# Every fourth low half of the weights by a negated copy and an adding transfer, in a transformer block written out without loops

## The chip, the core and the metric

The kernel runs on one core of one Trainium2 chip. The metric is the time of one execution in microseconds (us), the median of three runs. The core has TensorE (PE) for matmuls, VectorE (DVE), ScalarE (ACT), GpSimd (POOL) and SyncE (SP), which here only issues transfers. Each engine runs its own list of instructions in order; they meet at semaphores. Transfers run on the core's 16 DMA engines, issued by SP or by GpSimd.

## The reference

One block of a transformer on 256 tokens of width 2048, all in float32:

```python
xn = rms_norm(h, norm_mix_g[l])
proj = xn @ w_in[l]                       # 2048 x 8448
q_a, k_a, v_a, q_b, k_b, v_b, g_a, g_b = jnp.split(proj, offsets, axis=-1)
o_a = mixer_a(...)                        # 16 heads on 2 kv heads, window, sink, t5 bias
o_b = mixer_b(...)                        # 16 heads, chunked, relative bias
merged = sigmoid(g_a) * (o_a @ w_branch_a[l]) + sigmoid(g_b) * (o_b @ w_branch_b[l])
h = h + merged @ w_out[l]
hn = rms_norm(h, norm_ffn_g[l])
h = h + (silu(hn @ w_ffn_gate[l]) * (hn @ w_ffn_up[l])) @ w_ffn_down[l]   # width 5632
```

## The kernel before

All weights are read once from HBM, some 250 MB. To keep float32 accuracy each product is taken in three matmuls: weight and activation are each split into a high half (`w_hi`, `xT_hi`: the value rounded to the type float32r) and a low half (`w_lo`, `xT_lo`: what is left), and TensorE adds hi x hi, lo x hi and hi x lo in PSUM (lines 948, 949, 950).

The work is a list of jobs made by `plan`, one for each 512 columns of a weight (the first, `kv`, has 256). A job is a row of *pieces*: a piece is 2 x 128 rows of the weight by the job's columns, for TensorE 12 matmuls (2 row blocks, 2 token tiles, 3 products). There are 464 pieces, numbered through (`p`). Two pieces are a *chunk* of 1 MB, the unit of loading. For every piece each engine does its step, and then what `follow` hangs on that place in the list (taking sums out of PSUM, norms, gates, splitting the activations):

- SP loads chunk c into slot c % 4 of `raw` (line 394), when the low half of the last piece of chunk c - 4 is made (`lo_ready`).
- ScalarE copies the piece from `raw` to slot p % 4 of `w_hi` (`split_hi`, line 494), when TensorE is through with piece p - 4 (`piece_used`).
- VectorE subtracts: `w_lo` = `raw` - `w_hi` (`split_lo`, line 648).
- TensorE waits for `lo_ready` at the start of the piece and multiplies.

So `w_hi` and `w_lo` have four slots, and a piece may be made while TensorE works on the three before it. The jobs alternate between two pairs of PSUM banks. Between pieces TensorE also turns finished tiles (`turn_set`, line 877), and from the first `ga` job on (piece 72) it does attention for 34 pieces: on even pieces `scores` and `turn_probs`, on odd ones `values`, with exponentials on ScalarE (line 594) and maxima and scaling on VectorE. GpSimd has little to do: it issues eight small loads at the start and one small store (`bias_table_a`, line 469), and makes the reciprocal roots of the norms (`rsqrt`, lines 463 and 464), one for each of the seven jobs of kinds `kv` and `qk`, one for the input and one for the second norm.

The jobs of the merge (`gb`, `ba`, `bb`) and of the gate and up products are written as loops, with the counter added into semaphore values and addresses (`stepped`, `j.off`); the others are written out.

Of the kernel before, what the change touches and what calls it, by code (L numbers as in the profile page):

```python
# [32 lines left out]
CHUNK_KT = 4  # L33
RAW_SLOTS = 4
SPLIT_SLOTS = 4
BIAS_SLOTS = 4
FF_BLOCKS = 4
EPS = 1e-6
# [41 lines left out]
def plan(d, qa, kva, qb, dff):  # L80

    kt = d // P
    kb = qa // P
    jobs, segments = [], []
    turn = [0]

    def job(kind, n, weight, row0, col0, cols, kts, lhs, kt0, pair=None):
        if pair is None:
            pair = turn[0]
            turn[0] ^= 1  # L90
        jobs.append(Job(kind, n, weight, row0, col0, cols, kts, lhs, kt0, pair))
        return jobs[-1]

    b0 = qa + 2 * kva
    ga0 = b0 + 3 * qb
    job("kv", 0, "w_in", 0, qa, 2 * kva, kt, "x", 0)
    for n in range(qa // COLS):
        job("qk", n, "w_in", 0, n * COLS, COLS, kt, "x", 0)
    for n in range(2 * qb // COLS):
        job("qk", n + qa // COLS, "w_in", 0, b0 + n * COLS, COLS, kt, "x", 0)  # L100
    for n in range(qb // COLS):
        job("v", n, "w_in", 0, b0 + 2 * qb + n * COLS, COLS, kt, "x", 0)
    for n in range(d // COLS):
        job("ga", n, "w_in", 0, ga0 + n * COLS, COLS, kt, "x", 0)
    loops = []
    start = len(jobs)
    for n in range(d // COLS):
        job("gb", n, "w_in", 0, ga0 + d + n * COLS, COLS, kt, "x", 0, 0)
        job("ba", n, "w_branch_a", 0, n * COLS, COLS, kb, "o", 0, 1)
        job("bb", n, "w_branch_b", 0, n * COLS, COLS, kb, "o", kb, 2)  # L110
    loops.append((start + 3, 3, d // COLS - 1))
    turn[0] = 0
    for n in range(d // COLS):
        job("out", n, "w_out", 0, n * COLS, COLS, kt, "m", 0)
    blocks = dff // COLS
    down = 0
    for ff in range(0, blocks, FF_BLOCKS):
        k = min(FF_BLOCKS, blocks - ff)
        start = len(jobs)
        for n in range(k):  # L120
            job("gate", ff + n, "w_ffn_gate", 0, (ff + n) * COLS, COLS, kt, "h", 0)
            job("up", ff + n, "w_ffn_up", 0, (ff + n) * COLS, COLS, kt, "h", 0).slot = n
        loops.append((start + 2, 2, k - 1))
        for n in range(d // COLS):
            job("down", n, "w_ffn_down", ff * COLS, n * COLS, COLS, k * GROUP, "f", 0).done = down
            down += 1
    last_of, piece, sets = {}, 0, 0
    for a, j in enumerate(jobs):
        j.piece0 = piece
        piece += j.pieces  # L130
        j.prev = jobs[a - 1] if a else None
        j.before = last_of.get(j.pair)
        last_of[j.pair] = j
        if j.kind in ("qk", "kv", "bb", "out", "up"):
            j.set = sets
            sets += 1
    at = 0
    for start, width, count in loops:
        segments.append(jobs[at:start])
        segments.append((jobs[start:start + width], jobs[start + width:start + 2 * width], count))  # L140
        at = start + width * count
    segments.append(jobs[at:])
    return jobs, segments


def build(nc, x, norm_mix_g, w_in, q_norm_a, k_norm_a, sink_a, t5_bias, q_norm_b, k_norm_b, rel_bias_b,
# [21 lines left out]
    with ExitStack() as ctx:  # L168
# [87 lines left out]
        first_landed = sem("first_landed")  # L256
        landed = [sem(f"landed{i}") for i in range(RAW_SLOTS)]
        hi_ready = sem("hi_ready")
        lo_ready = sem("lo_ready")
        piece_used = sem("piece_used")  # L260
        x_landed = [sem(f"x_landed{i}") for i in range(NB)]
# [76 lines left out]
        def set_read(j):  # L338
# [2 lines left out]
                    "bb": lambda: (mT_ready, T * (j.n + 1)), "out": lambda: (scaled_ready, NB + j.n + 1),  # L341
                    "up": lambda: (fT_ready, T * (j.n + 1))}[j.kind]()

        def columns(j):
            return bass.ds(j.n * COLS, COLS) if not isinstance(j.n, int) else slice(j.n * COLS, (j.n + 1) * COLS)

# [30 lines left out]
        @block.sync  # L377
        def _(sp):
            x_view = x[0].rearrange("(t p) d -> p t d", p=P)
            out_view = out[0].rearrange("(t p) d -> p t d", p=P)  # L380

            def load_chunk(j, q):
                c = j.piece0 // 2 + q
                slot = c % RAW_SLOTS
                if c >= RAW_SLOTS:
                    sp.wait_ge(lo_ready, 2 * (c - RAW_SLOTS) + 2 + j.off)
                w = weights[j.weight]
                rows = slice(j.row0 + q * CHUNK_KT * P, j.row0 + (q + 1) * CHUNK_KT * P)
                src = w[0, rows, bass.ds(j.col0, j.cols)].rearrange("(k p) n -> p k n", p=P)
                dst = raw[:, slot, 0:CHUNK_KT * j.cols].rearrange("p (k n) -> p k n", n=j.cols)  # L390
                if c == 0:
                    sp.dma_start(dst[:, 0:PIECE_KT, :], src[:, 0:PIECE_KT, :]).then_inc(first_landed, 16)
                    dst, src = dst[:, PIECE_KT:, :], src[:, PIECE_KT:, :]
                sp.dma_start(dst, src).then_inc(landed[slot], 16)

            def load_bias(i):


                b, n = i % 2, i // 2
                slot = i % BIAS_SLOTS  # L400
                if i >= BIAS_SLOTS:
                    sp.wait_ge(scores_read, i - BIAS_SLOTS + 1)
                if b:
                    src, pitch, origin = rel_bias_b, rel_bias_b.shape[2], (rel_bias_b.shape[2] - 1) // 2 - ORIGIN
                    parts = ((0, 0, 4 * HD), (HP, 0, 3 * HD))
                else:
                    src, pitch, origin = table, REL, 0
                    parts = ((0, 2 * HD, 2 * HD), (HP, HD, 2 * HD))
                for p0, key0, keys in parts:
                    rows = bass.AP(src.tensor, src.offset + 2 * n * pitch + origin + p0 + key0,  # L410
                                   [[1, HP], [pitch, 2], [1, keys]])
                    sp.dma_start(bias[p0:p0 + HP, slot, :, key0:key0 + keys], rows).then_inc(bias_landed[slot], 16)

            def do_job(j):
                for q in range(j.pieces // 2):
                    if j.prev is None:
                        cs = slice(q * COLS, (q + 1) * COLS)
                        sp.dma_start(x_rows[:, :, cs], x_view[:, :, cs]).then_inc(x_landed[q], 16)
                    load_chunk(j, q)
                    i = att_step(j, 2 * q, 6)  # L420
                    if i >= 0 and i // 2 < NATT:
                        if i == 0:
                            sp.wait_ge(table_stored, 16)
                            sp.wait_ge(masks_ready, 1)
                        load_bias(i // 2)
                if j.kind == "bb" and j.first:
                    sp.wait_ge(o_ready, NATT)
                    sp.dma_start(h[:], x_view).then_inc(h_landed, 16)

            sp.dma_start(mix_rows[:], norm_mix_g[0].rearrange("(k p) -> k p", p=P)).then_inc(mix_landed, 16)  # L430
            run(sp, do_job)
            for n in range(NB):
                cs = slice(n * COLS, (n + 1) * COLS)
                sp.wait_ge(h_added, LAST_DOWN - NB + n + 2)
                sp.dma_start(out_view[:, :, cs], h[:, :, cs]).then_inc(out_stored, 16)
            sp.wait_ge(out_stored, 16 * NB)
# [3 lines left out]
        def _(pool):  # L440
# [22 lines left out]
                in_order(nc.gpsimd.tensor_scalar(mean, sums, 1.0 / n, EPS, ALU.mult, ALU.add))  # L463
                nc.gpsimd.tensor_tensor(dst, mean, minus_half[:, 0:width], ALU.pow).then_inc(ready, 1)

            pool.wait_ge(x_ss_ready, T)
            rsqrt(x_rs[:], x_ms[:], x_ss[:], D, T, x_rs_ready)
            pool.wait_ge(table_copied, 1)
            pool.dma_start(table, table_sb[:]).then_inc(table_stored, 16)
            for j in (j for j in jobs if j.kind in ("qk", "kv")):  # L470
                width = T * (j.cols if j.kind == "qk" else KVA) // HD
                pool.wait_ge(q_ss_ready, j.set + 1)
                if j.set:
                    pool.wait_ge(heads_normed, j.set)
                rsqrt(q_rs[:, 0:width], q_ms[:, 0:width], q_ss[:, 0:width], HD, width, q_rs_ready)
            pool.wait_ge(h_sum_ready, 1)
            rsqrt(h_rs[:], h_ms[:], h_sum[:], D, T, h_rs_ready)


        @block.scalar  # L480
        def _(act):
            A = nc.scalar.activation

            def split_hi(j, k):
# [6 lines left out]
                if p >= SPLIT_SLOTS:  # L491
                    act.wait_ge(piece_used, p - SPLIT_SLOTS + 1 + j.off)
                w = PIECE_KT * j.cols
                A(w_hi[:, p % SPLIT_SLOTS, 0:w], raw[:, c % RAW_SLOTS, (p % 2) * w:(p % 2 + 1) * w],  # L494
                  ACT.Copy).then_inc(hi_ready, 1)

            def out_of_psum(j, dst, cols, func=ACT.Copy, scale=x_rs):

# [135 lines left out]
        def _(dve):  # L634
# [8 lines left out]

            def split_lo(j, k):
                p = j.piece0 + k
                dve.wait_ge(hi_ready, p + 1 + j.off)
                w = PIECE_KT * j.cols
                V.tensor_tensor(w_lo[:, p % SPLIT_SLOTS, 0:w],  # L648
# [208 lines left out]
        def _(pe):  # L857
# [78 lines left out]
            def multiply(j, k):  # L936
                p = j.piece0 + k
                hi, lo = lhs[j.lhs]
                pe.wait_ge(lo_ready, p + 1 + j.off)
                for q in range(PIECE_KT):  # L940
                    kt = k * PIECE_KT + q
                    if kt % GROUP == 0:
# [74 lines left out]
```

## Time and profile before

| | |
|---|---|
| median of 3 runs (lowest to highest) | 1349.26 us (1349.22 to 1349.34) |
| span of the profiled execution, first to last instruction | 1347.3 us |
| TensorE, VectorE, ScalarE, GpSimd busy | 99%, 55%, 45%, 2% |
| granted TensorE clock, mean | 1.000 |
| moved by the DMA engines | 251.23 MB, mean 186 GB/s |

The profiled execution's own time is not given apart from its span; the median of the runs stands 2.0 us above that span, for what lies around the first and last instruction. Busy time counts instructions that compute, not waits. Matmuls are pipelined: each is shown with 0.39 us, but they start every 0.23 us, so TensorE counts as busy also across a short gap. A wait is put down to the engine or transfer whose semaphore came last.

### The profile page before, as it was taken

Reading aid. Unit: us, or ns where it says so; the run is one execution under the profiler, and the core shown is the slowest. Engines: PE = TensorE matmul, PEld = TensorE weight load, DVE = VectorE, ACT = ScalarE, POOL = GpSimd, SP = SyncE. Lnnn points to the kernel's source line nnn. Section 1 sums busy time; section 2 is a strip of 40 time slices with the busy share of each in tenths; the row PEclk is TensorE's granted clock in tenths of the full one; section 3 lists DMA queues with packets and bytes.
Section 4 is the critical chain, followed back from the end, with each engine's and each line's share of the span. In section 5 each row is a group of like instructions: output and inputs, shape, how many; then the busy total and the mean of one; then the engine's idle time right before and its main releaser. Section 6 shows DMA issues by size and latency. Waiting matters only on the chain.

```text
span 1347.3 us, 16021 instructions
## 1 busy us (share of the span) xinstructions
PE 1331.1 (99%) x6224; PEld 1100.3 (82%) x6224; DVE 743.3 (55%) x938; ACT 606.4 (45%) x781; POOL 33.5 (2%) x34
## 2 busy tenths in 40 slices
PE   7999999999999999999999999999999999999998
PEld 6888887777788888888888888888888888888887
DVE  6556556777455555565555555455545554555553
ACT  5454545555444444444444443344444434444442
POOL 1112110000000000000000000000000000000000
PEclk9999999999999999999999999999999999999999
DMA  8655655444565555555565555555555556555552
GB/s 260 198 202 165 210 188 182 147 148 143 206 200 188 188 187 188 188 185 187 188 193 185 191 188 201 194 188 188 189 186 188 187 200 196 195 187 187 187 187 94
DMA packets 129943, 251.23 MB, mean 186 GB/s; under 512 B 4624, under 2 KB 10832, under 8 KB 129632
## 3 DMA queue, kind: packets, MB, share of 16 engines
q1 hardware_dynamic: 129600, 250.37, 56.5%
q8 instruction: 38, 0.62, 0.2%
q0 software_dynamic: 288, 0.10, 0.1%
q14 instruction: 17, 0.14, 0.0%
HBM read 248.33 MB, written 2.12 MB: 186 GB/s over the span
## 4 chain that ended last, share of the span: by engine, by line
PE 95%; ACT 3%; DVE 1%; issue 0%; DMA 0%; DVEq 0%; SPq 0%; ACTq 0%
PE bank L948 30%; PE bank L950 30%; PE bank L949 30%; PE bank L877 2%; ACT prob L594 1%; PE bank L892 1%; ACT w_hi L494 1%; PE bank L917 1%; DVE staged L657 0%; PE bank L919 0%; PE bank L902 0%; DMA x_rows<-in_x 0%; PE bank L918 0%; DVE xT_lo L665 0%; DVE w_lo L648 0%
## 5 line engine op out<-in xcount | busy, mean ns | idle before, releaser
L648 DVE TENSOR_TENSOR w_lo<-raw,w_hi 128x1024 fp32r<-128x1024 f32 (+1 forms) x464 | 562.5, 1216 | 556.1 <-ACT w_hi L494 554.2
L494 ACT ACTIVATE w_hi<-raw 128x1024 fp32r<-128x1024 f32 (+1 forms) x464 | 487.6, 1052 | 694.8 <-PE bank L950 693.2
L948 PE MATMUL bank<-w_hi,xT_hi 128*128 128x512 f32 (+1 forms) x1248 | 488.6, 391 | 4.2 <-DVE w_lo L648 3.0
L950 PE MATMUL bank<-w_lo,xT_hi 128*128 128x512 f32 (+1 forms) x1248 | 483.2, 387 | 0.0
L949 PE MATMUL bank<-w_hi,xT_lo 128*128 128x512 f32 (+1 forms) x1248 | 482.9, 387 | 0.0
L948 PEld LDWEIGHTS bank<-w_hi,xT_hi 128*128 128x128 f32 x1248 | 234.9, 188 | 53.7 <-issue 2.6
L950 PEld LDWEIGHTS bank<-w_lo,xT_hi 128*128 128x128 f32 x1248 | 234.9, 188 | 47.9
L949 PEld LDWEIGHTS bank<-w_hi,xT_lo 128*128 128x128 f32 x1248 | 235.1, 188 | 45.8
L948 PE MATMUL bank<-w_hi,oT_hi 128*128 128x512 f32 x480 | 187.0, 390 | 0.0
L950 PE MATMUL bank<-w_lo,oT_hi 128*128 128x512 f32 x480 | 186.8, 389 | 0.0
L949 PE MATMUL bank<-w_hi,oT_lo 128*128 128x512 f32 x480 | 186.7, 389 | 0.0
L950 PEld LDWEIGHTS bank<-w_lo,oT_hi 128*128 128x128 f32 x480 | 90.1, 188 | 18.7
L949 PEld LDWEIGHTS bank<-w_hi,oT_lo 128*128 128x128 f32 x480 | 90.1, 188 | 18.6
L948 PEld LDWEIGHTS bank<-w_hi,oT_hi 128*128 128x128 f32 x480 | 90.1, 188 | 18.6
L948 PE MATMUL bank<-w_hi,mT_hi 128*128 128x512 f32 x128 | 50.2, 392 | 0.0
L950 PE MATMUL bank<-w_lo,mT_hi 128*128 128x512 f32 x128 | 49.9, 390 | 0.0
L949 PE MATMUL bank<-w_hi,mT_lo 128*128 128x512 f32 x128 | 49.8, 389 | 0.0
L594 ACT ACTIVATE prob<-prob,minus_top 128x128 f32<-128x128 f32 x64 | 28.1, 441 | 0.0
L950 PEld LDWEIGHTS bank<-w_lo,mT_hi 128*128 128x128 f32 x128 | 24.0, 188 | 5.0
L948 PEld LDWEIGHTS bank<-w_hi,mT_hi 128*128 128x128 f32 x128 | 24.0, 188 | 4.9
L949 PEld LDWEIGHTS bank<-w_hi,mT_lo 128*128 128x128 f32 x128 | 24.0, 188 | 4.9
L683 DVE TENSOR_TENSOR h<-bank,h 128x512 f32<-128x512 f32 x32 | 20.5, 682 | 8.5 <-PE bank L950 8.5
(109 smaller groups left out, 496.2 us busy)
## 6 DMA issues: line engine op xcount, KB each, us to landing
raw<-in_w_in SPq DMA_DIRECT2D x64, 1024.0 KB, 5.3
raw<-in_w_ffn_gate SPq DMA_DIRECT2D x44, 1024.0 KB, 5.2
raw<-in_w_ffn_up SPq DMA_DIRECT2D x44, 1024.0 KB, 5.1
raw<-in_w_ffn_down SPq DMA_DIRECT2D x44, 1024.0 KB, 5.0
raw<-in_w_out SPq DMA_DIRECT2D x16, 1024.0 KB, 5.0
raw<-in_w_branch_a SPq DMA_DIRECT2D x8, 1024.0 KB, 5.0
raw<-in_w_branch_b SPq DMA_DIRECT2D x8, 1024.0 KB, 4.9
x_rows<-in_x SPq DMA_DIRECT2D x4, 512.0 KB, 7.7
```

What stands on the lines that cost most here:

```text
L494: A(w_hi[:, p % SPLIT_SLOTS, 0:w], raw[:, c % RAW_SLOTS, (p % 2) * w:(p % 2 + 1) * w], ACT.Copy).then_inc(hi_ready, 1)
L594: A(v, v, ACT.Exp, bias=minus_top[:, s, q:q + 1], accum_out=row_sum[:, s, q:q + 1]).then_inc(exp_ready, 1)
L648: V.tensor_tensor(w_lo[:, p % SPLIT_SLOTS, 0:w], raw[:, p // 2 % RAW_SLOTS, (p % 2) * w:(p % 2 + 1) * w], w_hi[:, p % SPLIT_SLOTS, 0:w].bi ...
L683: ins = V.tensor_tensor(h[:, t, columns(j)], bank[2 * j.pair + t][:], h[:, t, columns(j)], ALU.add)
L877: ins = turn(bank[T_BANK + t][:, g * P:(g + 1) * P], src[:, t, g * P:(g + 1) * P], ident[:])
L892: ins = M(dst, qT[rows, b * PAIRS + n, tokens(t)], k, start=True, stop=True)
L917: M(bank[T_BANK][rows, 0:P], keys0, part[2], start=True, stop=True)
L948: M(sums, x_hi, w_hi[:, p % SPLIT_SLOTS, w], start=kt == 0, stop=False)
L949: M(sums, x_lo, w_hi[:, p % SPLIT_SLOTS, w], start=False, stop=False)
L950: ins = M(sums, x_hi, w_lo[:, p % SPLIT_SLOTS, w], start=False, stop=kt == j.kts - 1)
```

## The change

Two things. The loops go: `segments` becomes the one list of all jobs, so each engine's program is written out from start to end. And pieces with p % 4 == 3 (116 of 464) get their low half without VectorE: ScalarE, right behind the high half, writes `w_lo` = -`raw` rounded to float32r, that is, minus the high half; then GpSimd issues a transfer from `raw` to `w_lo`, SBUF to SBUF, that adds what it brings to what stands there. TensorE waits for the transfer's landing (`lo_summed`) on such a piece, and SP waits for it before it loads over the chunk. `lo_ready` counts the other pieces alone. GpSimd's rsqrt instructions now stand between its transfers, in the order of the pieces.

```diff
-    segments.append(jobs[at:])
+    segments = [jobs]
...
+        def by_dma(p):
+            return p % SUMMED == SUMMED - 1
+
+        def lo_by_dve(p):
+            return p + 1 - (p + 1) // SUMMED
...
                 if c >= RAW_SLOTS:
-                    sp.wait_ge(lo_ready, 2 * (c - RAW_SLOTS) + 2 + j.off)
+                    last = 2 * (c - RAW_SLOTS) + 1
+                    sp.wait_ge(lo_ready, lo_by_dve(last))
+                    if by_dma(last):
+                        sp.wait_ge(lo_summed, 16 * (last // SUMMED + 1))
...
+            def sum_lo(j, k):
+
+                p = j.piece0 + k
+                w = PIECE_KT * j.cols
+                pool.wait_ge(neg_ready, p // SUMMED + 1)
+                pool.dma_start(w_lo[:, p % SPLIT_SLOTS, 0:w],
+                               raw[:, p // 2 % RAW_SLOTS, (p % 2) * w:(p % 2 + 1) * w],
+                               accum_op=ALU.add).then_inc(lo_summed, 16)
...
+            def do_job(j):
+                for k in range(j.pieces):
+                    if by_dma(j.piece0 + k):
+                        sum_lo(j, k)
...
+                    if j.prev is not None and k == 3 and j.prev.kind in ("qk", "kv"):
+                        norm_heads(j.prev)
...
                 A(w_hi[:, p % SPLIT_SLOTS, 0:w], raw[:, c % RAW_SLOTS, (p % 2) * w:(p % 2 + 1) * w],
                   ACT.Copy).then_inc(hi_ready, 1)
+                if by_dma(p):
+                    A(w_lo[:, p % SPLIT_SLOTS, 0:w], raw[:, c % RAW_SLOTS, (p % 2) * w:(p % 2 + 1) * w],
+                      ACT.Copy, scale=-1.0).then_inc(neg_ready, 1)
...
             def split_lo(j, k):
                 p = j.piece0 + k
+                if by_dma(p):
+                    return
...
-                pe.wait_ge(lo_ready, p + 1 + j.off)
+                if by_dma(p):
+                    pe.wait_ge(lo_summed, 16 * (p // SUMMED + 1))
+                else:
+                    pe.wait_ge(lo_ready, lo_by_dve(p))
```

TensorE's instructions keep their order. How ScalarE's move is seen in a job of kind `qk`. Before, the eight high halves of a job (line 494), with the sums of the job before taken out after the fourth (line 500):

```order
L494 ACTIVATE w_hi<-raw 128x1024 [waits piece_used,landed0] x2
L494 ACTIVATE w_hi<-raw 128x1024 [waits piece_used,landed1] x2
L500 ACTIVATE side_a<-bank,x_rs 128x512 [waits heads_normed,piece_used]
L500 ACTIVATE side_a<-bank,x_rs 128x512
L494 ACTIVATE w_hi<-raw 128x1024 [waits piece_used,landed2] x2
L494 ACTIVATE w_hi<-raw 128x1024 [waits piece_used,landed3] x2
```

The same place after (line 526 is the old 494, line 535 the old 500):

```order
L526 ACTIVATE w_hi<-raw 128x1024 [waits piece_used,landed0] x2
L526 ACTIVATE w_hi<-raw 128x1024 [waits piece_used,landed1] x2
L529 ACTIVATE w_lo<-raw 128x1024
L535 ACTIVATE side_a<-bank,x_rs 128x512 [waits heads_normed,piece_used]
L535 ACTIVATE side_a<-bank,x_rs 128x512
L526 ACTIVATE w_hi<-raw 128x1024 [waits piece_used,landed2] x2
L526 ACTIVATE w_hi<-raw 128x1024 [waits piece_used,landed3] x2
L529 ACTIVATE w_lo<-raw 128x1024
```

The negated copy (line 529) stands behind the fourth and the eighth high half, ahead of the sums of the job before. GpSimd's list in the jobs of the heads, before:

```order
L463 TENSOR_SCALAR q_ms<-q_ss 128x4 [waits q_ss_ready]
L464 TENSOR_TENSOR q_rs<-q_ms,minus_half 128x4 [waits pool_step]
L463 TENSOR_SCALAR q_ms<-q_ss 128x16 [waits heads_normed,q_ss_ready]
L464 TENSOR_TENSOR q_rs<-q_ms,minus_half 128x16 [waits pool_step]
L463 TENSOR_SCALAR q_ms<-q_ss 128x16 [waits heads_normed,q_ss_ready]
```

And after (line 483 issues the adding transfer; 475 and 476 are the old 463 and 464):

```order
L483 DMA w_lo<-raw 128x1024 [waits neg_ready]
L475 TENSOR_SCALAR q_ms<-q_ss 128x4 [waits q_ss_ready]
L476 TENSOR_TENSOR q_rs<-q_ms,minus_half 128x4 [waits pool_step]
L483 DMA w_lo<-raw 128x1024 [waits neg_ready] x2
L475 TENSOR_SCALAR q_ms<-q_ss 128x16 [waits heads_normed,q_ss_ready]
L476 TENSOR_TENSOR q_rs<-q_ms,minus_half 128x16 [waits pool_step]
L483 DMA w_lo<-raw 128x1024 [waits neg_ready] x2
```

Two transfers stand between one norm and the next, each behind ScalarE's negated copy. SP's loads, whose waits change at every second chunk, after:

```order
L406 DMA raw<-in_w_in 128x4x512 [waits lo_ready]
L406 DMA raw<-in_w_in 128x4x512 [waits lo_summed,lo_ready]
L406 DMA raw<-in_w_in 128x4x512 [waits lo_ready]
L406 DMA raw<-in_w_in 128x4x512 [waits lo_summed,lo_ready]
L406 DMA raw<-in_w_in 128x4x512 [waits lo_ready]
```

Before, each of them waited for `lo_ready` alone.

## Rows read from the trace of the kernel before

**Rows 1.** The page: span, and each engine's busy time, its share, and instructions

```profile
span 1347.3 us, 16021 instructions
...
PE 1331.1 (99%) x6224; PEld 1100.3 (82%) x6224; DVE 743.3 (55%) x938; ACT 606.4 (45%) x781; POOL 33.5 (2%) x34
```

**Rows 2.** The page: the chain that ended last, by engine

```profile
PE 95%; ACT 3%; DVE 1%; issue 0%; DMA 0%; DVEq 0%; SPq 0%; ACTq 0%
```

**Rows 3.** Waits of TensorE: who waited for whom; us in total, times, longest

```profile
PE bank L867 <- DMA x_rows<-in_x: 6.9, 2, 5.9
PE bank L948 <- DVE w_lo L648: 3.0, 4, 1.6
PE bank L948 <- ACT gate_a L500: 1.2, 1, 1.2
```

**Rows 4.** Windows: stretch, length, busy of PE, PEld, DVE, ACT, POOL; clock, DMA share, GB/s

```profile
16.00:26.00 10.00, 9.55 (x76) 8.59 (x73) 7.75 (x11) 6.59 (x10) 0.00 (x0) 1.00 0.79 259
26.00:30.00 4.00, 3.26 (x25) 2.93 (x24) 3.21 (x9) 4.00 (x5) 1.47 (x3) 1.00 0.50 129
...
100.00:200.00 100.00, 100.00 (x459) 83.12 (x458) 56.30 (x48) 47.02 (x53) 16.02 (x8) 1.00 0.57 185
...
900.00:1000.00 100.00, 100.00 (x451) 82.97 (x450) 53.45 (x51) 43.67 (x46) 0.00 (x0) 1.00 0.58 190
```

**Rows 5.** Timeline, ScalarE and TensorE near 905 us: start, us, instruction

```profile
904.02 1.06 ACT L494 ACTIVATE w_hi<-raw 128x1024 fp32r<-128x1024 f32 x1 [0.50 <-PE bank L950]
906.74 1.06 ACT L494 ACTIVATE w_hi<-raw 128x1024 fp32r<-128x1024 f32 x1 [1.66 <-PE bank L950]
909.46 1.06 ACT L494 ACTIVATE w_hi<-raw 128x1024 fp32r<-128x1024 f32 x1 [1.66 <-PE bank L950]
...
906.48 0.39 PE L948 MATMUL bank<-w_hi,xT_hi 128*128 128x512 f32 x1
```

**Rows 6.** The page, costliest groups: count, busy, mean ns, idle before and its releaser

```profile
L648 DVE TENSOR_TENSOR w_lo<-raw,w_hi 128x1024 fp32r<-128x1024 f32 (+1 forms) x464 | 562.5, 1216 | 556.1 <-ACT w_hi L494 554.2
```

**Rows 7.** Timeline of GpSimd, one rsqrt of a head job

```profile
57.62 1.10 POOL L463 TENSOR_SCALAR q_ms<-q_ss 128x16 f32<-128x16 f32 x1 [21.10 <-DVE q_ss L698]
58.81 2.90 POOL L464 TENSOR_TENSOR q_rs<-q_ms,minus_half 128x16 f32<-128x16 f32 x1
```

**Rows 8.** The chain in order of time (three pieces), and ScalarE's timeline

```profile
1.20 4.55 DMA x_rows<-in_x
...
5.88 1.94 PE bank L867 x8
...
1061.71 0.87 PE bank L877 x8
...
27.76 3.89 ACT L494 ACTIVATE w_hi<-raw 128x1024 fp32r<-128x1024 f32 x4
```

**Rows 9.** Timeline of VectorE behind the ScalarE copy of 906.74

```profile
907.84 1.23 DVE L648 TENSOR_TENSOR w_lo<-raw,w_hi 128x1024 fp32r<-128x1024 f32 x1 [1.49 <-ACT w_hi L494]
```

**Rows 10.** Transfers by line: issuer, count, KB each, median us from issue to landing

```profile
raw<-in_w_in SPq DMA_DIRECT2D x64, 1024.0 KB, 5.3
...
bias<-bias_table_a SPq DMA_DIRECT2D x16, 64.0 KB, 4.9
...
t_hot<-in_onehot POOLq DMA_DIRECT2D x1, 48.0 KB, 6.1
bias_table_a<-table_sb POOLq DMA_DIRECT2D x1, 24.0 KB, 4.6
mix_rows<-in_norm_mix_g SPq DMA_DIRECT2D x1, 8.0 KB, 1.7
```

**Rows 11.** The page, DMA queues: packets, MB, share of 16 engines over the span

```profile
q1 hardware_dynamic: 129600, 250.37, 56.5%
```

**Rows 12.** Timeline of ScalarE in attention, the even pieces

```profile
246.10 1.06 ACT L494 ACTIVATE w_hi<-raw 128x1024 fp32r<-128x1024 f32 x1 [2.50 <-PE bank L950]
...
254.49 1.06 ACT L494 ACTIVATE w_hi<-raw 128x1024 fp32r<-128x1024 f32 x1 [3.48 <-PE bank L950]
```

**Rows 13.** Timeline of TensorE near 16 us, matmuls of 256 columns

```profile
14.89 0.41 PE L949 MATMUL bank<-w_hi,xT_lo 128*128 128x256 f32 x1
15.11 0.41 PE L950 MATMUL bank<-w_lo,xT_hi 128*128 128x256 f32 x1
...
16.53 0.28 PE L950 MATMUL bank<-w_lo,xT_hi 128*128 128x256 f32 x1
16.65 0.28 PE L948 MATMUL bank<-w_hi,xT_hi 128*128 128x256 f32 x1
```

More of the change, by code:

```diff
@@ L35 @@
 SPLIT_SLOTS = 4
+SUMMED = 4
 BIAS_SLOTS = 4
@@ L258, in build @@
         hi_ready = sem("hi_ready")
+        neg_ready = sem("neg_ready")
+        lo_summed = sem("lo_summed")
         lo_ready = sem("lo_ready")
@@ L464, in rsqrt, with norm_heads @@
                 nc.gpsimd.tensor_tensor(dst, mean, minus_half[:, 0:width], ALU.pow).then_inc(ready, 1)
[L466 to L470, printed above, removed]
+            def sum_lo(j, k):
[5 more added lines that the diff above has]
+                               accum_op=ALU.add).then_inc(lo_summed, 16)
+            def norm_heads(j):
                 width = T * (j.cols if j.kind == "qk" else KVA) // HD
@@ L475, in _ @@
                 rsqrt(q_rs[:, 0:width], q_ms[:, 0:width], q_ss[:, 0:width], HD, width, q_rs_ready)
-            pool.wait_ge(h_sum_ready, 1)
-            rsqrt(h_rs[:], h_ms[:], h_sum[:], D, T, h_rs_ready)
+            def do_job(j):
+                for k in range(j.pieces):
+                    if by_dma(j.piece0 + k):
+                        sum_lo(j, k)
+                    if j.prev is None and k == j.pieces - 1:
+                        pool.wait_ge(x_ss_ready, T)
+                        rsqrt(x_rs[:], x_ms[:], x_ss[:], D, T, x_rs_ready)
+                        pool.wait_ge(table_copied, 1)
+                        pool.dma_start(table, table_sb[:]).then_inc(table_stored, 16)
+                    if j.prev is not None and k == 3 and j.prev.kind in ("qk", "kv"):
+                        norm_heads(j.prev)
+                    if j.prev is not None and k == 5 and j.prev.kind == "out" and j.prev.n == NB - 1:
+                        pool.wait_ge(h_sum_ready, 1)
+                        rsqrt(h_rs[:], h_ms[:], h_sum[:], D, T, h_rs_ready)
+            run(pool, do_job)
         @block.scalar
```

## The prediction, written before the result was known

> **What bounds the kernel now.** I read the page's shares first. TensorE is busy for 99% of a span of 1347.3 us, VectorE for 55%, ScalarE for 45%, GpSimd for 2% [rows 1]; the chain that ended last is 95% TensorE, and most of that by the three matmul lines 948 to 950, which are that engine's weight products [rows 2]. Then the waits of TensorE: 6.9 us for the input rows at the start, 3.0 us for `w_lo`, 1.2 us for a gate [rows 3]. So nothing that another engine does in less time can shorten the middle of the run. Last the pace. In a stage written without loops (100 to 200 us) and in one that is a loop (900 to 1000 us) TensorE is busy for the whole 100 us at full granted clock [rows 4], and ScalarE's high halves, one for each piece, start at 904.02, 906.74 and 909.46 us [rows 5]: one piece of weights (12 matmuls of 512 columns) takes 2.72 us. There are 464 pieces, and 464 x 2.72 = 1262 us are the floor of this kernel; the rest is attention, turning of tiles, start and end.
>
> **The change, part by part.** Every fourth piece (index 3, 7, ... 463: 116 of the 464) gets its low half in another way.
>
> *Loops.* Written out, they would give something only if TensorE stopped at their edges. It does not: the loop stage of rows 4 has no hole, and no wait of rows 3 is at a branch. 0 us, either way; I see no mechanism that would make long straight code slower, since the first 100 us stretch of rows 4 is straight code.
>
> *VectorE* loses 116 subtractions of 1216 ns (141 us of busy time) [rows 6]. It waits 556.1 us for ScalarE before these instructions already [rows 6], so this buys 0.
>
> *ScalarE* gains 116 copies like the 1.06 us one of rows 5, some 122 us, on 606 us of busy time in 1347. As a load it fits. On the path it counts in the chain below. In attention the exponentials follow the high half of an even piece, while the new copy follows an odd one (the index leaves 3 when divided by 4), and only the small `split_o` is behind it; 0 there.
>
> *GpSimd* issues the 116 transfers. What is queued behind each is the next rsqrt, and ahead of it the last one; an rsqrt takes 1.10 + 2.90 us [rows 7] and comes once in each of eight jobs, right behind the transfer of piece 3, while the next is wanted four pieces (10.9 us) later. That fits.
>
> *The chain of one transferred piece* is what decides. Piece p can't be touched before TensorE is through with piece p - 4, whose slot it takes (there are four), and TensorE must have it three pieces later. Counted from the moment at which TensorE starts on p - 3 (call it 0): ScalarE's high half starts at 0.26 (906.48 is the first matmul of a piece, 906.74 the copy, [rows 5]). The negated copy follows it on the same engine; four such copies in a row take 3.89 us, so the second starts 0.94 us after the first and ends after 0.94 + 1.06 = 2.00 us, at 2.26 [rows 5, 8]. GpSimd gets it some 0.05 us later (VectorE starts 0.03 us after the copy that it waits for, 906.74 + 1.06 to 907.84, [rows 5, 9]). Then X, the transfer from issue to landing, and 0.13 us until TensorE runs (the input rows landed at 1.20 + 4.55 = 5.75, TensorE started at 5.88, [rows 8]). Together 2.44 + X. TensorE has three pieces to do in that time, 8.16 us, so **the transfer is free up to X = 5.7 us**. Above that TensorE stands still once in four pieces, for X - 5.7, and it does not catch up: the next transferred piece can start only when this one's slot is used.
>
> *X* is in no row, so I bound it. Fixed part: GpSimd's own small transfers need 4.6 to 6.1 us from issue to landing; the one that leaves SBUF when the start is over, 24 KB, needs 4.6 us, while the smallest one of SP needs 1.7 [rows 10]. I take 4.6, with 1.7 and 6.1 as ends. Data part: the queue of SP moved 250.37 MB in 56.5% of the span [rows 11], 0.565 x 1347.3 / 250.37 = 3.04 us for each MB. The transfer writes 0.52 MB but must read both `raw` and `w_lo`, 1.05 MB: 3.2 us. The ends are 1.6 us (only the bytes written count) and 6.4 us (the adding halves the pace). So X lies between 1.7 + 1.6 = 3.3 and 6.1 + 6.4 = 12.5, and I take 4.6 + 3.2 = 7.8 us, because the 24 KB transfer is the nearest row: GpSimd's queue, SBUF as source, loads of weights beside it.
>
> The Trainium skill ("DMA: Bandwidth & Descriptors", section "Anatomy of one DMA") gives 2.0 us + bytes / 436 GB/s for a transfer issued by GpSimd, that is, as its estimate, 3.2 us for 512 KB and 4.4 us for twice that, either of them free here. This case's trace does not agree for the small one: by that rule 24 KB would take 2.1 us, and the row has 4.6. I go by the row. The same skill ("Collectives: The Full Stack", on why reduce-scatter is slower) says that an adding transfer pays for its two source reads and not for the add; no run here shows that yet.
>
> *Collisions.* Two weight loads of 1 MB go in each four pieces (5.3 us and less to landing, [rows 10]). They now wait for the transfer at every second chunk, and both leave when it lands; 2.1 MB by 3.04 us are 6.4 us of data, so they are mostly through when the next transfer is issued (2.72 + 2.31 = 5.0 us after TensorE starts on the piece that landed) and its fixed part has gone by. What they bring is wanted four pieces later at the earliest. Busy time of the DMA engines for four pieces: 6.4 + 3.2 = 9.6 us of 13.0. It fits, without much room. On SP's queue the bias loads of attention now stand behind chunk loads that wait for the transfer; they are issued six pieces ahead of their use (over 20 us there) and take some 5 us [rows 10], so nothing waits for them.
>
> *The sum.* A stall of 7.8 - 5.7 = 2.1 us. Attention hides it: there a pair of pieces takes 8.4 us (copies at 246.10 and 254.49, [rows 12]), so three pieces last more than 12 us, and 9 of the groups lie there. The first two groups are in the first job with half-wide pieces, where the start is bound by the input; I put 5 us on them for two transfers that nothing can cover. 116 - 9 - 2 = 105 groups x 2.1 = 220 us. Off that goes the time in which TensorE turns tiles between pieces, which lengthens the cover: 0.87 us [rows 8] in each of 26 jobs (7 heads, 4 + 4 merges and outputs, 11 hidden blocks), 23 us. 220 - 23 + 5 = +202 us on the span of 1347.3. The median of the runs is 1349.26, 2.0 us above the span for what lies around it, which stays: **1551 us**.
>
> **The rivals.**
>
> *A: the transfer is hidden, no slower.* One mechanism: X at or below 5.7 us. Then every wait is met and TensorE's floor is the time: 1349 us, plus up to 5 at the start. For it: fixed 1.7 + data 3.2 = 4.9, if GpSimd's queue is as quick as SP's. Against it: no transfer of GpSimd's in the trace lands in less than 4.6, and 1.1 us is too little for any 512 KB here. At 5.7 us it decides. A gain has no mechanism at all, as TensorE has the same matmuls and 11 us of waits in all to lose, none of them at what is changed but 3.0. (The rule of the Trainium skill cited above, on the same page, would make it this case.)
>
> *B: the adding transfer is slow.* X = 11 (4.6 + 6.4) makes the stall 5.3: 105 x 5.3 - 23 + 5 = +539, 1888 us. At X = 12.5 it is 105 x 6.8 - 23 + 5 = +696, 2045 us. For it: nothing shows the pace of an addition. Against it: the DMA engines would be busy 6.4 + 6.4 of 16 us only, so it would have to come from the adding itself.
>
> *C: the clock.* TensorE is at 1.2 GHz until some 15 us (matmuls of 256 columns start each 0.21 us) and at 2.4 GHz from then on (0.12 us) [rows 13]. Nothing shows whether a stop of 2 us in 13 brings it back. If it did for good, a piece would take about 12 x 0.43 = 5.1 us, and 464 x 2.4 = +1100, 2450 us. I hold it unlikely: the input-bound first job, with TensorE busy for 9.55 of the 10 us from 16 to 26 us and 3.26 of the next 4, left it up [rows 4].
>
> *D: less than I think.* X = 6.2 (4.6 + 1.6), a stall of 0.5: 105 x 0.5, less the part of the 23 that counts, +5: about 1400 us.
>
> **How the numbers follow.** The forecast's own mechanism (X from 6.5 to 10, 1450 to 1780 us) 0.63; D 0.11; A 0.11; B (X above 10 us) 0.13; C 0.02. The range goes from 1385, which leaves out A, to 1900 (X = 11.1), which takes in half of B; some 0.19 lie outside. About 0.2% (2.7 us) is what a measurement can tell from no change: faster 0.02, same 0.07, slower 0.91; a part of A is slower by the start.
>
> **What will show it.** In the profile after: the group of the transfers with its landing time, 7.8 us if I am right, 5.7 or less if A; TensorE's wait for that landing at some 105 places, 2 us each and missing from about 210 to 340 us; ScalarE's copies four to a group, with one interval of 4.8 us and three of 2.7; clock at 1.0 throughout. I am wrong if TensorE waits for something else (a weight load, ScalarE, VectorE), or if the stage from 900 us on still runs at 2.72 us a piece.

## The result, and the profile after

The changed kernel takes 1372.7 us in the median of 4 runs (1370.36 to 1377.66), the kernel before 1349.26: a ratio of 1.0179 [1.0167, 1.0191], +23.4 us. The profiled execution took 1371.98 us, with a span of 1370.2. The sign was forecast, the size was not: 1551 us, with a range from 1385 to 1900.

The page after: span, busy time, the chain by engine, and the DMA queues (q0 is GpSimd's, q1 SP's).

```profile
span 1370.2 us, 15415 instructions
...
PE 1339.5 (98%) x6224; PEld 1103.1 (81%) x6224; DVE 608.4 (44%) x822; ACT 712.5 (52%) x897; POOL 133.1 (10%) x150
...
q1 hardware_dynamic: 129600, 250.37, 53.0%
q0 software_dynamic: 16992, 60.40, 23.2%
...
PE 87%; DMA 6%; ACT 4%; issue 3%; DVE 1%; POOL 0%; DVEq 0%; SPq 0%; ACTq 0%; POOLq 0%
...
L483 POOL DMA_DIRECT2D w_lo<-raw x116 | 100.3, 865 | 1200.8 <-ACT w_lo L529 1178.6
...
w_lo<-raw POOLq DMA_DIRECT2D x114, 512.0 KB, 4.6
```

VectorE lost 135 us of busy time and ScalarE gained 106 against [rows 1], where I had worked out 141 and 122. 6% of the chain is now in DMA. The last row is the one that matters: the transfer lands 4.6 us after its issue, where I had taken 7.8. Up to 5.7 it costs nothing, by the sum of the prediction.

The waits of TensorE after, for matmuls and for weight loads (us in total, times, longest), against [rows 3]:

```profile
PE bank L988 <- DMA w_lo<-raw: 13.8, 11, 4.1
PE bank L904 <- DMA x_rows<-in_x: 7.0, 2, 6.2
PE bank L988 <- ACT gate_a L535: 2.1, 1, 2.1
PE bank L988 <- DVE w_lo L685: 1.8, 1, 1.8
...
PEld bank L988 <- DMA w_lo<-raw: 19.3, 14, 4.6
```

TensorE waits for the transfer at 14 places of 116, not at 105. Where the time is lost is seen by the start of one and the same high half, on ScalarE, in both traces; how much later it starts after the change I call the lag. Pieces 12, 71, 119 and 463, before:

```profile
33.27 1.06 ACT L494 ACTIVATE w_hi<-raw 128x1024 fp32r<-128x1024 f32 x1 [0.61 <-PE bank L950]
199.70 1.06 ACT L494 ACTIVATE w_hi<-raw 128x1024 fp32r<-128x1024 f32 x1 [1.66 <-PE bank L950]
379.04 1.06 ACT L494 ACTIVATE w_hi<-raw 128x1024 fp32r<-128x1024 f32 x1 [1.66 <-PE bank L950]
1332.01 1.06 ACT L494 ACTIVATE w_hi<-raw 128x1024 fp32r<-128x1024 f32 x1 [1.66 <-PE bank L950]
```

and after:

```profile
38.67 1.06 ACT L526 ACTIVATE w_hi<-raw 128x1024 fp32r<-128x1024 f32 x1 [1.19 <-PE bank L990]
213.29 1.06 ACT L526 ACTIVATE w_hi<-raw 128x1024 fp32r<-128x1024 f32 x1 [2.53 <-PE bank L990]
400.49 1.06 ACT L526 ACTIVATE w_hi<-raw 128x1024 fp32r<-128x1024 f32 x1 [7.67 <-PE bank L990]
1354.42 1.06 ACT L526 ACTIVATE w_hi<-raw 128x1024 fp32r<-128x1024 f32 x1 [1.66 <-PE bank L990]
```

The lag is 5.4, 13.6, 21.5 and 22.4 us. So 5.4 us are lost in the first job, 8.2 in the jobs of the heads, 7.9 from attention to the first merge, 6.0 of them at one transfer, and 1.0 us in the 344 pieces that follow. In that last part the landings are short: from 410 us on their minimum, median and maximum, and the same from 40 to 215 us, in this order:

```profile
DMA to landing us min/median/max: 4.5/4.6/6.0
DMA to landing us min/median/max: 4.5/6.0/8.2
```

Two of the slow places, by the timelines of SP and GpSimd (start, us, instruction). In the heads:

```profile
70.81 0.37 SPq L406 DMA_DIRECT2D raw<-in_w_in  x1
71.39 0.91 POOL L483 DMA_DIRECT2D w_lo<-raw  x1 [3.01 <-ACT w_lo L529]
79.57 0.50 PE L988 MATMUL bank<-w_hi,xT_hi 128*128 128x512 f32 x1 [1.50 <-DMA w_lo<-raw]
79.59 0.92 SPq L406 DMA_DIRECT2D raw<-in_w_in  x2
```

and at the first merge, where the wait is longest (the row with DMA alone is from the chain: start, us):

```profile
379.62 0.37 SPq L406 DMA_DIRECT2D raw<-in_w_branch_b  x1
380.04 0.51 SPq L440 DMA_DIRECT2D h<-in_x  x1
380.59 0.47 SPq L406 DMA_DIRECT2D raw<-in_w_in  x1
385.90 9.86 DMA w_lo<-raw
395.82 0.92 SPq L406 DMA_DIRECT2D raw<-in_w_in  x2
```

A load of 1 MB set out 0.58 us ahead of the transfer of 71.39, which landed 8.1 us after its issue. 4 MB set out from 379.6 us on; the first of them had landed when the transfer of 385.90 was issued, 3 were under way, and it needed 9.9 us. Far from any of them, in the long last part:

```profile
903.79 0.86 POOL L483 DMA_DIRECT2D w_lo<-raw  x1 [10.02 <-ACT w_lo L529]
908.35 1.29 SPq L406 DMA_DIRECT2D raw<-in_w_ffn_up  x2
```

Here both loads of a group set out when the transfer has landed, 4.56 us after its issue. The second is not quite over when the next one is issued: it set out at 909.27 and landed at 916.07, the next transfer was issued at 914.67, and it landed in 4.5 us all the same. My sum had this picture; in the heads it does not hold. There the loads alternate: one group has both behind the landing, in the next one of them sets out 0.6 to 1.4 us ahead of the transfer, and those transfers (pieces 23, 31, 39, 47, 55, 63) land in 6.2 to 8.2 us.

What such a load does is seen in the transfers of each DMA queue in the first 4 us after the issue (packets, MB, share of the 16 engines). After 71.39 the engines move SP's bytes alone, and no packet of the transfer:

```profile
q1 hardware_dynamic: 400, 0.82, 86.3%
```

After 903.79 they have moved all of the transfer's 0.52 MB in that time:

```profile
q0 software_dynamic: 128, 0.52, 68.5%
```

The first packet runs 1.4 us after the issue at 903.79, 4.4 us after it at 71.39, and 4.5 us after it at 385.90.

Why the load is late is in VectorE's list. The load of 70.81 waits for the low half of piece 21, and that one stands behind the scaling of the heads, which waits for GpSimd's reciprocal root:

```profile
68.42 1.23 DVE L744 TENSOR_TENSOR staged<-side_a,q_rs 128x1024 f32<-128x1024 f32 x1 [3.11 <-POOL q_rs L476]
69.56 1.22 DVE L685 TENSOR_TENSOR w_lo<-raw,w_hi 128x1024 fp32r<-128x1024 f32 x1
```

The low half ends at 70.78, the load is issued at 70.81.

The clock was touched too: windows after, columns as in [rows 4] (the third from the end is the granted clock).

```profile
30.57:37.40 6.83, 5.97 (x20) 5.30 (x21) 1.96 (x2) 3.27 (x7) 0.65 (x1) 0.50 0.71 238
395.80:399.21 3.41, 3.41 (x8) 2.73 (x9) 0.00 (x0) 0.00 (x0) 0.00 (x0) 0.50 0.65 193
```

0.50 is the lower of the two levels (1.2 GHz). The first stretch begins within the wait of 3.2 us in the first job, which ends at 31.4 us; the second follows the wait of 4.1 us that ends at 395.8. At half the clock they cost, as an estimate, 3 us and 1.7 us of work.

### The profile page after: what moved, and what is told of

Its sections match the earlier page's. It is cut to its first block, busy times and chain, and to the rows that moved or that the text cites. A ratio compares the mean times of both kernels' runs of the same rounds, so it can differ in the third digit from the quotient of the medians.

```text
span 1370.2 us, 15415 instructions
## 1 busy us (share of the span) xinstructions
PE 1339.5 (98%) x6224; PEld 1103.1 (81%) x6224; DVE 608.4 (44%) x822; ACT 712.5 (52%) x897; POOL 133.1 (10%) x150
## 3 DMA queue, kind: packets, MB, share of 16 engines
q0 software_dynamic: 16992, 60.40, 23.2%
## 4 chain that ended last, share of the span: by engine, by line
PE 87%; DMA 6%; ACT 4%; issue 3%; DVE 1%; POOL 0%; DVEq 0%; SPq 0%; ACTq 0%; POOLq 0%
PE bank L988 28%; PE bank L990 27%; PE bank L989 27%; DMA w_lo<-raw 5%; ACT w_hi L526 1%; PE bank L914 1%; ACT prob L629 1%; PE bank L929 1%; ACT w_lo L529 1%; PE bank L954 1%; PE bank L956 0%; DMA x_rows<-in_x 0%; PE bank L939 0%; PE bank L955 0%; ACT probT L635 0%
## 5 line engine op out<-in xcount | busy, mean ns | idle before, releaser
L685 DVE TENSOR_TENSOR w_lo<-raw,w_hi 128x1024 fp32r<-128x1024 f32 (+1 forms) x348 | 422.2, 1216 | 613.0 <-ACT w_hi L526 610.6
L483 POOL DMA_DIRECT2D w_lo<-raw x116 | 100.3, 865 | 1200.8 <-ACT w_lo L529 1178.6
L529 ACT ACTIVATE w_lo<-raw 128x1024 fp32r<-128x1024 f32 (+1 forms) x116 | 119.9, 1034 | 0.0
L781 DVE SCALAR_TENSOR_TENSOR side_b<-bank,h_rs,side_a 128x512 f32<-128x512 f32 x22 | 15.5, 747 | 33.2 <-ACT side_a L616 33.2
```

What stands on the lines that cost most here:

```text
L483: pool.dma_start(w_lo[:, p % SPLIT_SLOTS, 0:w], raw[:, p // 2 % RAW_SLOTS, (p % 2) * w:(p % 2 + 1) * w], accum_op=ALU.add).then_inc(lo_sum ...
L529: A(w_lo[:, p % SPLIT_SLOTS, 0:w], raw[:, c % RAW_SLOTS, (p % 2) * w:(p % 2 + 1) * w], ACT.Copy, scale=-1.0).then_inc(neg_ready, 1)
L685: V.tensor_tensor(w_lo[:, p % SPLIT_SLOTS, 0:w], raw[:, p // 2 % RAW_SLOTS, (p % 2) * w:(p % 2 + 1) * w], w_hi[:, p % SPLIT_SLOTS, 0:w].bi ...
L781: V.scalar_tensor_tensor(side_b[:, t, :], bank[2 * j.pair + t][:], h_rs[:, t:t + 1], side_a[:, t, :], ALU.mult, ALU.mult).then_inc(gate_re ...
```

## The experiments

Times are medians; each ratio is to the kernel before, run beside it on the same chip (its medians there are 1349.10 to 1349.14).

**Loops alone.** No piece goes by transfer.

```diff
         def by_dma(p):
-            return p % SUMMED == SUMMED - 1
+            return False
         def lo_by_dve(p):
-            return p + 1 - (p + 1) // SUMMED
+            return p + 1
```

> The loops are written out, and every low half is still made by VectorE's subtraction; nothing is transferred. Theory (all of the +23 us comes from waits for the adding transfer): same as before within 0.2%, 1347 to 1352 us, no wait of TensorE longer than before. Rival (straight code itself costs, for example in fetching instructions): part of the +23 us shows here, 1355 us or more, with waits of TensorE that nothing releases.

1349.67 us, ratio 1.0004 [0.9994, 1.0013]. Straight code adds 0.5 us, which the interval does not tell from nothing; the rest of the 23 us comes from the other part.

**A copy in place of the addition.** The transferred low halves are wrong here, so this run serves the times alone.

```diff
-                               accum_op=ALU.add).then_inc(lo_summed, 16)
+                               ).then_inc(lo_summed, 16)
```

> The transfer copies raw to w_lo instead of adding to it, so the low halves of every fourth piece are not low halves. Theory (the adding transfer pays for two source reads, 2.7 us of data on 1.8 us of fixed part): an undisturbed landing falls from 4.5 to about 3.2 us, and the queue's share of the DMA engines falls by half, 23% to about 12%; the time falls to some 1355 to 1365 us, since a shorter transfer is hit by a load less often. Rival 1 (what costs is what GpSimd does ahead of the data, whose length goes with the rows): landing stays at 4.3 to 4.5 us. Rival 2 (the adding itself is slow): landing falls below 2.8 us.

1356.0 us, ratio 1.0051 [1.0031, 1.0071]. GpSimd's queue takes 12.5% of the DMA engines, and the landings from 410 us on are:

```profile
q0 software_dynamic: 16992, 60.40, 12.5%
...
DMA to landing us min/median/max: 2.9/2.9/5.4
```

The addition costs 1.6 us of landing and doubles the time on the engines (23.2% of 1370 us over 116 transfers is 2.74 us each, 12.5% of 1353 us is 1.46). That is what a second read of the same size would cost, as the theory said. Landing was 2.9 and not 3.2, near the bound of the second rival. The issuing instruction is shorter too, 0.53 us on GpSimd in place of 0.86. These 0.33 us and the 1.28 us of engine time make up the 1.6; but no run has the second read without the addition, so how much is the adding itself stays open.

**VectorE adds.** ScalarE's copy stays, GpSimd does nothing.

```diff
+                if by_dma(p):
+                    dve.wait_ge(neg_ready, p // SUMMED + 1)
+                    lo = w_lo[:, p % SPLIT_SLOTS, 0:w]
+                    V.tensor_tensor(lo, raw[...], lo.bitcast(F32), ALU.add).then_inc(lo_ready, 1)
+                    return
```

> ScalarE makes the negated copy as in the change, but VectorE adds raw to it, so no transfer is issued. Theory (ScalarE's extra 120 us are covered, only the transfer is waited for): 1348 to 1353 us. Rival (the extra copy delays the evacuations, the gates and the next high halves on ScalarE): 1355 to 1365 us, with waits of TensorE for ScalarE or for w_lo.

1359.7 us, ratio 1.0078 [1.0058, 1.0098]: a miss. In the heads nothing is lost, the lag of the high halves stays at 1.0 to 1.2 us from piece 12 to piece 64; so ScalarE's copy is covered there, and the 8.2 us of the change in that stage are the transfer's. From piece 81 to piece 105, beside attention, the lag grows from 1.7 to 5.5 us, and TensorE waits for VectorE:

```profile
PE bank L939 <- DVE oT_lo L841: 3.6, 7, 0.8
```

Here VectorE can start on an odd piece only after the second copy of ScalarE, a microsecond late, with the maxima and `oT_lo` queued behind. The change has no such wait on VectorE, and its one wait for `oT_lo` is 0.8 us; so this run says nothing of ScalarE's cost in attention under the change. At piece 108 the lag is 8.0 us: the first gate, behind the negated copy, makes TensorE wait 2.1 us here (1.2 before), and 3.4 us at the lower clock follow. Another 2.6 us are lost from piece 120 to piece 174.

**Two halves in a row.** Each transfer is two of 256 KB, the second issued when the first has landed.

```diff
+                for part, done in ((0, half_summed), (1, lo_summed)):
+                    c0, c1 = part * w // 2, (part + 1) * w // 2
+                    if part:
+                        pool.wait_ge(half_summed, 16 * (p // SUMMED + 1))
+                    pool.dma_start(w_lo[..., c0:c1], raw[..., c0:c1], accum_op=ALU.add).then_inc(done, 16)
```

> Each transfer is issued as two halves of 256 KB, the second when the first has landed. Theory (fixed part 1.8 us, data 2.7 us for the whole, free up to 5.7 us): each half lands in about 3.15 us, together 6.4 us, a stall of 0.7 us for each of some 105 groups less what the turning of tiles covers: 1372 + 50 = 1410 to 1440 us. If the fixed part were the 4.6 us that I took, the two would need 12 us and the time would be over 1900 us. If the free time is larger than 5.7 us, the time stays near 1375 us.

1599.2 us, ratio 1.1853 [1.1829, 1.1877]. The waits, the landings from 410 us on, and one group (the high half of piece 147, its two issues, TensorE's start):

```profile
PE bank L993 <- DMA w_lo<-raw: 178.8, 107, 6.4
...
DMA to landing us min/median/max: 3.2/3.3/8.4
...
529.53 1.06 ACT L531 ACTIVATE w_hi<-raw 128x1024 fp32r<-128x1024 f32 x1 [3.35 <-PE bank L995]
...
531.83 0.86 POOL L488 DMA_DIRECT2D w_lo<-raw  x1 [7.87 <-ACT w_lo L534]
535.80 0.86 POOL L488 DMA_DIRECT2D w_lo<-raw  x1 [3.11 <-DMA w_lo<-raw]
539.12 0.50 PE L993 MATMUL bank<-w_hi,oT_hi 128*128 128x512 f32 x1 [1.53 <-DMA w_lo<-raw]
```

This is the test of the chain. The issue comes 2.30 us after the high half starts (my sum: 2.31 less 0.26, 2.05), TensorE starts 7.29 us after the issue, and its wait is 1.53 us, so the free time is 7.29 - 1.53 = 5.76 us to the start, 5.6 to the landing, where I had 5.7. And with a transfer that long, TensorE does wait in nearly each group: its matmuls wait 107 times, 178.8 us in all, which is near the +202 us that I forecast for 7.8. The model of the stall is right; the expectation here fell short since the two halves took 7.3 us (3.97 from issue to issue, 3.3 to land) in place of 6.4, and the clock fell to a mean of 0.970, some 48 us of work. The sizes: 256 KB land in 3.3 us and 512 KB in 4.5 to 4.6, so the data part is 2 x 1.25 = 2.5 us and the fixed part 2.0 to 2.1.

**Loads behind the transfer.** Each weight load waits for the next landing.

```diff
-                    if by_dma(last):
-                        sp.wait_ge(lo_summed, 16 * (last // SUMMED + 1))
+                    sp.wait_ge(lo_summed, 16 * (last // SUMMED + 1))
```

> As the change, but every weight load waits for the landing of the adding transfer that comes next, so no load sets out just before or during a transfer. Theory (from 35 to 215 us TensorE waits because a load, held up by VectorE's head norms, is on the DMA engines together with the transfer, which then lands in 6 to 8 us instead of 4.5): the slow landings there go, the 8 us lost in that stage go, 1362 to 1366 us in all. Rival (the transfers of that stage are slow because of GpSimd's or VectorE's own work beside them): landings of 6 to 8 us stay, time 1370 us or more; or the later loads now starve ScalarE, 1380 us or more.

1395.7 us, ratio 1.0337 [1.0319, 1.0355]: the time is where a rival had put it, over 1380; what was expected of the heads held. Landings from 40 to 215 us, and the windows (columns as above):

```profile
DMA to landing us min/median/max: 4.5/4.6/5.3
...
35.00:215.00 180.00, 180.00 (x820) 149.21 (x820) 80.75 (x70) 98.17 (x113) 39.59 (x30) 1.00 0.79 235
215.00:400.00 185.00, 160.22 (x874) 126.11 (x873) 92.22 (x316) 97.50 (x235) 8.63 (x10) 0.94 0.54 153
```

In the heads no landing is slow and TensorE has no hole; the lag there stays at 4.3 us from piece 21 to piece 64, where the change went from 5.4 to 12.0. Same ScalarE, GpSimd and VectorE work, other times of the loads: the slow landings come from the loads. What was lost instead is in attention (the lag goes from 4.3 to 37.1 us between pieces 78 and 108), by a wait I had seen and called free: bias loads stand behind the held weight loads on SP's queue. VectorE waits for them, and ScalarE hardly at all for weights (1.0 us in the whole run), so it is not the late weight loads that starve attention.

```profile
DVE prob L809 <- DMA bias<-in_rel_bias_b: 25.1, 7, 4.1
PE bank L938 <- DVE oT_lo L840: 17.0, 6, 3.4
```

**The load of h in four.** One quarter behind each `bb` job.

```diff
-                if j.kind == "bb" and j.first:
-                    sp.wait_ge(o_ready, NATT)
-                    sp.dma_start(h[:], x_view).then_inc(h_landed, 16)
+                if j.kind == "bb":
+                    if j.first:
+                        sp.wait_ge(o_ready, NATT)
+                    sp.dma_start(h[:, :, columns(j)], x_view[:, :, columns(j)]).then_inc(h_landed, 16)
```

> As the change, but the 2 MB load of the block's input for the residual is cut into four of 512 KB, one behind each job of the merge. Theory (that load is on the DMA engines together with the transfer issued at 386 us, which lands in 9.9 us; a wait of 4.1 us and 3.4 us at the low clock follow): the long wait near 386 us and the drop of the clock go, 5 to 6 us less, 1365 to 1368 us. Rival (the loss there is ScalarE's table load and sigmoids behind the negated copy): the wait stays.

1368.8 us, ratio 1.0146 [1.0126, 1.0166], 3.9 us less than the change. The longest matmul wait for a transfer fell from 4.1 to 3.1 us, and that one is in the first job:

```profile
PE bank L989 <- DMA w_lo<-raw: 9.8, 13, 3.1
```

At piece 119 the lag grows by 0.9 us, not 6.0; so the load of `h` was the cause. Some comes back: the transfers issued 5.3 to 5.9 us behind the later quarters land in 5.5 to 6.6 us, and from piece 132 to piece 212 the lag grows from 17.4 to 20.1 us (it stays within 0.7 us of 22 in the change).

**The first job subtracted.**

```diff
         def by_dma(p):
-            return p % SUMMED == SUMMED - 1
+            return p >= 2 * SUMMED and p % SUMMED == SUMMED - 1
```

> As the change, but pieces 3 and 7, in the first job, are subtracted by VectorE as before; 114 transfers are left. Theory (the wait of 3.2 us for the transfer of piece 7 and the 6.8 us at the low clock after it cost 5 us): 5 us less, 1366 to 1369 us, clock 1.0 from 20 us on. Rival (the next transfer, of piece 11, meets the same and the loss only moves): no less than 1370 us.

1369.75 us, ratio 1.0153 [1.0133, 1.0173], 2.9 us less: as predicted in place, smaller in size. At piece 15 the lag is 1.6 us in place of 5.4, at piece 67 7.8 in place of 12.7. Of these 4.9 us some go again at the first gate (piece 108: 11.7 against 15.4): TensorE waits 2.1 us for it in both, but here 3.4 us at the lower clock follow. The rest goes at the load of `h` and behind piece 212.

**All three.** The edits of the last three together.

> The three edits together. Theory (the three places are all but some 3 us of the 23 us): 1350 to 1355 us, still not below the kernel before, since TensorE's own work is the floor. Rival (the places are not independent: what is given back at one is taken at the next transfer): 1358 us or more.

1392.2 us, ratio 1.0317 [1.03, 1.0334]: a miss. The lag is 0.8 us at piece 61, and 32 us at piece 104: the bias loads again. The expectation was written before the result with all loads held was known, and falls with it.

**Loads held outside attention.** The three edits, but the loads of pieces 72 to 121 go as in the change.

```diff
+                    upto = last if HELD0 <= 2 * c < HELD1 or by_dma(last) else last + 2
+                    if N_DMA[upto]:
+                        sp.wait_ge(lo_summed, 16 * N_DMA[upto])
```

> The three edits together, but the loads of pieces 72 to 121, beside which SP issues attention's bias loads, wait as in the change and not for the landing that comes next. Theory (what the held loads cost was the bias loads standing behind them on SP's queue, some 33 us in attention; outside it they only take collisions away): the 33 us go, the gain of 8 us from 35 to 215 us stays, and so do those of the first job and of the load cut in four: 1353 to 1359 us. Rival (the late weight loads themselves starve attention, or the gain is lost at the next stage): over 1362 us.

1363.0 us, ratio 1.01 [1.0083, 1.0117]. The 33 us are gone and the heads stay clean (lag 0.5 us at piece 61). But the time is above my range and past the 1362 us of the rival, 4 to 10 us more than I expected: 3.4 us around pieces 67 to 81, where held and free loads meet and the first bias loads come, 2.5 to piece 108, 3.4 more to piece 245, and 4 at the end, where a transfer beside the stores lands in 7.6 us and 3.4 us at the lower clock follow.

**And attention subtracted.** As the last, and pieces 75 to 111 by VectorE.

```diff
+SKIP0, SKIP1 = 72, 112
+        BY_DMA = [p >= 2 * SUMMED and p % SUMMED == SUMMED - 1 and not SKIP0 <= p < SKIP1 for p in ...]
```

> As the other kernel of this call, and pieces 75 to 111, those beside attention, are subtracted by VectorE as before (104 transfers are left). Theory (beside attention the change costs 2 to 3 us: the negated copy in front of the gate on ScalarE and slow landings among the bias loads): 2 to 3 us less than the other, 1350 to 1356 us, with no wait of TensorE over 1 us between 215 and 345 us; still not below 1349 us, the time of TensorE's own work. Rival (VectorE's relief in attention is worth something): no less than the other.

1356.8 us, ratio 1.0059 [1.0043, 1.0076], 6.2 us less than the last, where I expected 2 to 3. From piece 78 to piece 118 the lag stays at 2.0 to 2.6 us, where the last run went from 2.1 to 6.4: some 4 of the 6 us. The rest lies outside attention, where both have the same code, and I can't tell it from what differs between executions (1354.4 to 1357.9 us here, 1360.8 to 1365.4 there). This is the best form with transfers, and it is slower than the kernel before. Its waits:

```profile
PE bank L996 <- DMA w_lo<-raw: 2.9, 2, 1.6
...
PE bank L996 <- ACT gate_a L543: 1.2, 1, 1.2
```

The gate costs 1.2 us again as in [rows 3]. In every run with the negated copy ahead of it, it costs 2.1 or 2.2. No version beats the kernel before.

## Why the prediction was wrong

*The bound, the loops, VectorE.* Right. TensorE's pace stayed 2.72 us a piece, from 900 us on too, which the prediction had named as a sign of being wrong; straight code adds 0.5 us, and VectorE's relief bought nothing.

*ScalarE and GpSimd.* Right in the heads and later. At the end of attention there was a cost that I put at 0: the gate behind the negated copy, 0.9 us more than before, and, as an estimate, 1.7 us on top where the lower clock follows.

*The chain.* Right: 2.30 us to the issue and some 5.6 us free, against 2.05 and 5.7. The run with two halves in a row shows the stall for a transfer that exceeds it.

*X, the step that failed: "I take 4.6, ... because the 24 KB transfer is the nearest row".* X is 4.5 us: 2.0 fixed and 2.5 of data. My data part, 3.2, was near. The fixed part was mis-sized by 2.6 us, and the row that I took it from was not undisturbed. Before, SP issued a load of 1 MB just ahead of that transfer: it was issued at 28.91 us, 0.84 us behind the load, landed 4.6 us later [rows 10], and in the first 3 us the engines moved SP's packets alone. After the change no load set out in the 6 us ahead of it; an adding transfer of GpSimd's own was under way. The load before, the adding transfer after, and the landing after:

```profile
28.07 0.37 SPq L394 DMA_DIRECT2D raw<-in_w_in  x1
...
26.46 0.86 POOL L483 DMA_DIRECT2D w_lo<-raw  x1 [7.97 <-ACT w_lo L529]
...
bias_table_a<-table_sb POOLq DMA_DIRECT2D x1, 24.0 KB, 2.4
```

The 1.7 us of the smallest transfer on SP was the better bound. The rule that I set aside, 2.0 us + bytes / 436 GB/s (the Trainium skill, "DMA: Bandwidth & Descriptors", section "Anatomy of one DMA"), gives, as its estimate, 4.4 us for the two reads, against 4.5 measured, and 2.1 for 24 KB, against 2.4 with no load ahead. And what the Trainium skill says of adding transfers ("Collectives: The Full Stack", section "The bandwidth ceiling", that the second read is what costs) agrees with the time on the engines, 2.74 against 1.46 us.

*Collisions, put at nothing.* Wrong: they are some 16 of the 22.4 us of lag (8.2 in the heads, 6.0 at the load of `h`, 1.0 at the first bias loads, 1.0 in the last part); 5.4 are the first job and 0.9 the gate. With X at 4.5 and 5.6 us free there is 1.1 us to spare, and a load that sets out 0.6 to 1.4 us ahead takes it (landings of 6.2 to 8.2 us). My check asked whether the bytes of a group fit into its time, and whether the loads that leave at the landing are over by the next issue. It did not ask when the other load of the group leaves. That one waits for `lo_ready` of VectorE; in the heads it left 0.58 us ahead of a transfer. The trace shows what makes it late, the head norms ahead of the low half on VectorE; no run changes them. That the load is the cause of the slow landing is shown by the run that holds the loads. The bias loads, for which "nothing waits", were waited for once, 3.8 us by VectorE, and in the run with the loads held they cost 33 us.

*The rivals.* It was rival A (X below 5.7, the time near 1349 us) by mechanism, at 0.11, with a cost that A did not have; that the first job cost 5.4 us where I had put 5 is luck in part, as those 5 had no sum behind them. No run supports B. C was right in kind and small: the clock did fall at single long waits, for 3.4 to 6.8 us, and came back.

## What to carry to other kernels

A latency read from one row is that of its surroundings: look up what was on the same engines when it was issued, before it stands as a fixed cost. When a new transfer has a deadline, compare its slack with the length of each load that can be ahead of it, and not only the bytes with the bandwidth; and where loads are held back to make room, see what else stands behind them on the same issuing queue. If the engine that bounds the kernel hardly waits for the work that is moved (3.0 us of 1347 here), there is next to nothing to gain by moving it.

## What the runs showed of the hardware

A transfer of 512 KB from SBUF to SBUF, issued by GpSimd, lands 2.9 us after its issue as a copy and 4.5 us when it adds to its destination; 256 KB that add land in 3.3 us. Its issue takes 0.86 us of GpSimd when it adds, for either size, and 0.53 us as a copy.

Beside a load of SP's that set out just ahead, GpSimd's transfer did not share the DMA engines evenly from the start. With a load of 1 MB issued 0.58 us ahead, its first packet ran 4.4 us after its issue, in place of 1.4, and it landed in 8.1 us; the load landed in 6.3. With 3 MB under way it was 4.5 and 9.9 us.

A wait of TensorE of 3.2 us in the first job had 6.8 us at 1.2 GHz with it, one of 4.1 us had 3.4 us. The wait of 2.1 us for the first gate was followed by 3.4 us at 1.2 GHz in four runs (VectorE adds, `h` in four, first job subtracted, loads held outside) and by none in the change and in the copy without addition. With waits of 1.7 us in nearly each group, as in the run with two halves in a row, the mean stayed at 0.970.
